# A two-layer decoder trunk: layers written out, one weight split moved ahead, another order of the first loads, a shorter last stage

## The chip, the cores and the metric

The kernel runs on one core of a Trainium2 chip. The time is the device time of one execution in microseconds (us); less is better. Five engines take part: TensorE (PE, matrix products into PSUM), VectorE (DVE), ScalarE (ACT), GpSimd (POOL) and SyncE (SP, which here only issues transfers). They run separate instruction streams and meet in semaphores.

## The reference

One inference step of a two-layer decoder for 256 prompt tokens and 8 sample tokens (264 columns in all), model width 1024, everything in float32:

```python
for l in range(2):
    h = h + 0.5 * rmsnorm(swiglu(rmsnorm(h, g1), wg1, wu1, wd1), p1)   # 1024 -> 2816 -> 1024
    a = rmsnorm(h, gm) @ w_in
    y = concat(conv_module(a), multiscale_pool(a), sparse_attention(a, caches)) @ w_out
    h = h + rmsnorm(y, pm)
    h = h + 0.5 * rmsnorm(swiglu(rmsnorm(h, g2), wg2, wu2, wd2), p2)
return h, new keys, values, conv and pool states of each layer
```

## The kernel before

**Data.** The activations stand transposed: `h[:, d, :]` is the residual, 128 features by 264 columns for each of eight `d`. The weights come as *units* of 128x1024 float32 (512 KB): 156 for each layer. A feed-forward part (ffn) uses 66 of them (22 gate and 22 up, in turns, then 22 down), the mixer 24.

**Three products for one.** A unit lands in `raw` (6 buffers). ACT copies it to `w_hi` in a rounded format, DVE computes `w_lo = raw - w_hi`; both have 3 buffers. This pair is called `split(L, u)`: it waits for the unit in `raw` and for PE to be done with the unit three earlier (`split_free`). PE then runs 24 matmuls per unit (`three`: x_hi·w_hi, x_lo·w_hi, x_hi·w_lo, for eight `d`).

**A stage.** Each of the six parts (ffn, mixer, ffn, twice) begins with `first_units` on PE: for each `d` in `ORDER` a column sum of squares and the products of the part's first two units. So PE works while `x_hi` (ACT), `x_lo` (DVE) and the squares `sq` come in. Meanwhile `rstd` becomes ready: ACT a square root from PSUM, DVE a reciprocal. In an ffn DVE then runs `gate(0)` (gs = product times rstd), ACT `silu(0)`, both the split of the fourth unit, `split(L, u0 + 3)`, DVE `up(0)`, and after them a loop of 7 rounds over the other units. POOL multiplies gate and up (`mid`).

**The end of a stage** is `post(L, n, ...)`: ACT squares the eight outputs, DVE adds them in pairs, PE sums them (`post_sums`) and then runs WARM = 9 products of constants; ACT takes the square root (`rms_post`), DVE the reciprocal and then for each `d` y = output * gain * rstd_post, POOL adds `h += y` (`add`), ACT and DVE make the next part's `x_hi`, `sq`, `x_lo` (`pre`, `pre_lo`). ACT and DVE also split two further units in `post`.

**Order.** On each engine the order is that in which the code is written. The loop over the layers is a loop on the chip (`Fori(0, DEPTH)`) on PE, ACT, DVE and POOL, in which semaphore values are computed from the register L (`at_layer`); on SP it is written out. The last layer therefore ends as any other: x_hi, x_lo, squares and column sums of a next layer are computed, three units (`TAIL`) behind the last one are loaded, and POOL reloads the parameters `pars`. At the end SP stores `h[:, d, :]` to `yT` as `h_new` counts up.

**The start.** SP issues `pars`, `h` as one transfer of 1056 KB, a table of ones, four units, three tables, two units. ACT waits for the first three of these (`inputs` at 48) and unit 0, splits units 0, 1, 2, and then makes the eight `x_hi` and `sq`.

Of the kernel before, what the change touches and what calls it, by code (L numbers as in the profile page):

```python
# [14 lines left out]
AL = mybir.AluOpType  # L15
ACT = mybir.ActivationFunctionType
# [5 lines left out]
NT = NP + NB  # L22
# [45 lines left out]
ORDER = (0, 1, 7, 2, 3, 4, 5, 6)  # L68
WARM = 9
# [19 lines left out]
    step=400,  # L89
# [6 lines left out]
def build(nc, xT, wts, par, cst, ptab, digits, kT, vC, kxT, scT, spT,  # L96
          yT, okT, ovT, okiT, ocP, ocS, opP, opS):
    ctx = ExitStack()
    with ctx:
# [119 lines left out]
        result = ctx.enter_context(nc.semaphore("result"))  # L219
        vx_full = ctx.enter_context(nc.semaphore("vx_full"))  # L220
# [22 lines left out]
        def _(sp):  # L243
# [37 lines left out]

            sp.dma_start(pars[:, :], par[0]).then_inc(inputs, 16)
            sp.dma_start(h[:, :, :], xT).then_inc(inputs, 16)
            sp.dma_start(con[:, C_ONE:C_COS], cst[:, C_ONE:C_COS]).then_inc(inputs, 16)
            for n in range(4):
                unit(n)
# [6 lines left out]
            for L in range(DEPTH):  # L293
                n = L * UNITS + RAW
                places = {}

                def read(*sequences):
                    for b in sequences:
                        places[b] = [page(g + b * NPG) for g in range(NPG)]


                with sp.Fori(0, NPG) as g:
                    for j in range(RAW):
                        unit(n + j, g)
# [24 lines left out]
                for q in range(KV):  # L329
                    batch(kT, L, q, places[2 * q + 1], "k_used", q + 1)  # L330

                sp.wait_ge(sem["unit_done"], at_layer(L, "unit_done", U_MIX + N_IN - 1))
                first_values(L, 0, places)
                spare_values(L, 2, places)
                batch(vC, L, 3, places[7], "k_used", KV + 4)

                sp.wait_ge(sem["v_used"], at_layer(L, "v_used", 2))
                for n in range(end, L * UNITS + U_FFN2):
                    unit(n)
                n = L * UNITS + U_FFN2  # L340
                last = (L + 1) * UNITS + (RAW if L + 1 < DEPTH else TAIL)
                with sp.Fori(0, (last - n) // RAW) as i:
                    for j in range(RAW):
                        unit(n + j, i)
                for n in range(last - (last - n) % RAW, last):
                    unit(n)

            for i, d in enumerate(ORDER):
                sp.wait_ge(sem["h_new"], at_layer(DEPTH - 1, "h_new", SIGNALS["h_new"] - KD + i + 1))
                sp.dma_start(yT[:, d, :], h[:, d, :]).then_inc(result, 16)  # L350
# [14 lines left out]
        def _(act):  # L365
# [22 lines left out]
            def post(L, n, nxt):  # L388
                for d in range(KD):
# [6 lines left out]
                    if d == 0:  # L396
                        act.activation(y[:, 0, :], PS[:, 0, 0:NT], ACT.Copy).then_inc(sem["y_out"], 1)
                    act.activation(sq[:, d, :], PS[:, d, 0:NT], ACT.Square).then_inc(sem["sq_post"], 1)
                split(L, (U_FFN, U_FFN2, UNITS)[n] + 1)
# [4 lines left out]
                               scale=four / D, bias=epsb[:, at:at + 1]).then_inc(sem["rms_post"], 1)  # L404
                pre(L, 8 * n, nxt, (U_FFN, U_FFN2, UNITS)[n] + 2)
                warm(1 + n, ACT.Tanh if n == 0 else ACT.Silu)

            def ffn(L, u0, f0):
# [8 lines left out]

                silu(0)
                split(L, u0 + 3)
# [13 lines left out]
                split(L, u0 + 66)  # L433
# [112 lines left out]
            act.wait_ge(inputs, 48)  # L546
            act.wait_ge(setup, 1)
            for u in range(TAIL):
                act.wait_ge(raw_full[u], 16)
                act.activation(w_hi[:, u, :], raw[:, u, :], ACT.Copy).then_inc(sem["w_hi"], 1)  # L550
            for d in ORDER:
                act.activation(x_hi[:, d, :], h[:, d, :], ACT.Copy,
                               scale=pars[:, PRE1 + d:PRE1 + d + 1]).then_inc(sem["x_hi"], 1)
                act.activation(sq[:, d, :], h[:, d, :], ACT.Square).then_inc(sem["sq_pre"], 1)  # L554
# [3 lines left out]
            with act.Fori(0, DEPTH) as L:  # L558
                ffn(L, 0, 0)
                post(L, 0, PREM)  # L560
                mixer(L)
                post(L, 1, PRE2)
                ffn(L, U_FFN2, KF)
                post(L, 2, PRE1N)
# [3 lines left out]
        def _(dve):  # L568
# [28 lines left out]
            def post(L, n, gain, nxt):  # L597
# [3 lines left out]
                split(L, (U_FFN, U_FFN2, UNITS)[n] + 1)  # L601
                dve.wait_ge(sem["rms_post"], at_layer(L, "rms_post", n + 1))
                after(L, step(L, dve.reciprocal(rstd_post[:, :], rstd_post[:, :])))

                for i in range(KD + 2):
# [10 lines left out]
            def ffn(L, n, u0, f0):  # L616
# [22 lines left out]
                dve.wait_ge(sem["rstd"], at_layer(L, "rstd", n))  # L639
                gate(0)  # L640
                split(L, u0 + 3)
# [14 lines left out]
                split(L, u0 + 66)  # L656
# [367 lines left out]
            dve.wait_ge(inputs, 48)  # L1024
            for u in range(TAIL):
                dve.wait_ge(raw_full[u], 16)
                dve.wait_ge(sem["w_hi"], u + 1)
                tt(w_lo[:, u, :], raw[:, u, :], w_hi[:, u, :].bitcast(F32), AL.subtract).then_inc(sem["w_lo"], 1)
            for i, d in enumerate(ORDER):
                dve.wait_ge(sem["x_hi"], i + 1)  # L1030
# [10 lines left out]
            with dve.Fori(0, DEPTH) as L:  # L1041
# [10 lines left out]
        def _(pe):  # L1052
# [19 lines left out]
            def post_sums(L, n):  # L1072
# [5 lines left out]

                pe.wait_ge(tables, 48)
# [360 lines left out]
            pe.wait_ge(inputs, 48)  # L1440
            with pe.Fori(0, DEPTH) as L:
# [6 lines left out]
            for i, d in enumerate(ORDER):  # L1448

                if i == 0:  # L1450
                    pe.wait_ge(sem["y_new"], at_layer(DEPTH, "y_new", 3 - KD))
                pe.wait_ge(sem["sq_pre"], DEPTH * SIGNALS["sq_pre"] + i + 1)
                pe.matmul(PS[:, 7, 0:NT], ones, sq[:, d, :],
                          start=(i == 0), stop=(i == KD - 1)).then_inc(sem["mm_pre"], 1)


        @block.gpsimd
        def _(pool):
# [11 lines left out]
            def add(L, n):  # L1470

                for i, d in enumerate(ORDER):
                    pool.wait_ge(sem["y_new"], at_layer(L, "y_new", 8 * n + i + 1))
# [11 lines left out]
            with pool.Fori(0, DEPTH) as L:  # L1485
# [45 lines left out]

                pool.wait_ge(sem["x_lo"], at_layer(L, "x_lo", 24))
# [126 lines left out]
```

## Time and profile before

| | |
|---|---|
| median of 3 runs | 1177.87 us (1174.03 to 1178.01) |
| the profiled execution: its own time | 1174.9 us |
| its span, first to last instruction | 1173.0 us |
| PE busy | 1095.5 us (93% of the span) |
| DVE, ACT, POOL busy | 757.0, 531.7, 209.2 us |
| mean granted TensorE clock | 0.980 of full |
| HBM read | 189.35 MB, 164 GB/s over the span |

The profile is one execution. The time of an engine in which it waits is given with what ended the wait; where nothing is seen that ended it, the row says "issue". Times in rows count from the start of the span. A matmul of 264 columns is shown with its pipelined duration (0.28 us at full clock, 0.42 at half); what counts is the distance between starts, 0.12 us at full clock.

### The profile page before, as it was taken

The numbers are of one execution on the slowest core, as the hardware profiler recorded it, in microseconds if no ns is written. First come the engines' busy times: TensorE is split into PE (matmuls) and PEld (weight loads), VectorE is DVE, ScalarE is ACT, GpSimd is POOL, SyncE is SP. The second block draws the span as 40 slices with busy tenths as digits, with TensorE's granted clock in tenths as the row PEclk, the third lists the DMA queues.
The fourth block names the chain that finished last, engine by engine and source line by source line (L and its number), as shares of the span: only waits on it lengthen the run. The fifth ranks groups of instructions, "written<-read, shape, count | busy, mean of one in ns | idle before, by whom it ended". The sixth has DMA issues, their size and how long they took to land.

```text
span 1173.0 us, 28793 instructions
## 1 busy us (share of the span) xinstructions
PE 1095.5 (93%) x9404; PEld 1034.2 (88%) x9404; DVE 757.0 (65%) x1250; ACT 531.7 (45%) x856; POOL 209.2 (18%) x245
## 2 busy tenths in 40 slices
PE   4999999999679999999989999999986799999997
PEld 4999999987458999999979999998864799999995
DVE  4666654689965666664466666448889466666546
ACT  5444433631444544443464444345215555444335
POOL 3112200411300221210041221004222022122002
PEclk9999999999979999999999999999998899999999
DMA  7445655443565355555434565563347535555541
GB/s 255 174 166 187 228 192 205 156 136 125 147 88 182 110 186 178 181 188 179 159 95 169 185 228 179 205 225 122 121 134 128 147 105 180 179 179 179 189 169 39
DMA packets 90506, 192.91 MB, mean 164 GB/s; under 512 B 12338, under 2 KB 48370, under 8 KB 90306
## 3 DMA queue, kind: packets, MB, share of 16 engines
q1 hardware_dynamic: 87426, 186.39, 49.1%
q0 software_dynamic: 3008, 5.60, 2.2%
q8 instruction: 40, 0.66, 0.3%
q14 instruction: 32, 0.26, 0.1%
HBM read 189.35 MB, written 2.59 MB: 164 GB/s over the span
## 4 chain that ended last, share of the span: by engine, by line
PE 50%; issue 39%; DVE 4%; POOLq 2%; ACT 2%; POOL 2%; DMA 1%; DVEq 0%; ACTq 0%; SPq 0%
PE PS L1055 14%; PE PS L1056 14%; PE PS L1057 14%; PE PS L1161 3%; PE PS L1089 2%; POOLq L1519 1%; POOL vx L1520 1%; PE PS L1104 1%; PE PS L1101 1%; PE PS L1100 1%; POOL h L1474 1%; ACT w_hi L369 1%; POOLq L1520 1%; DVE w_lo L576 1%; DVE wk L701 1%
## 5 line engine op out<-in xcount | busy, mean ns | idle before, releaser
L576 DVE TENSOR_TENSOR w_lo<-raw,w_hi 128x1024 fp32r<-128x1024 f32 x300 | 394.7, 1316 | 314.1 <-ACT w_hi L369 312.4
L1055 PE MATMUL PS<-x_hi,w_hi 128*128 128x264 f32 x1456 | 416.9, 286 | 10.5 <-DVE w_lo L576 10.5
L369 ACT ACTIVATE w_hi<-raw 128x1024 fp32r<-128x1024 f32 x300 | 315.6, 1055 | 242.9 <-PE PS L1057 219.0
L1056 PE MATMUL PS<-x_lo,w_hi 128*128 128x264 f32 x1456 | 414.6, 285 | 0.0
L1057 PE MATMUL PS<-x_hi,w_lo 128*128 128x264 f32 x1456 | 414.3, 285 | 0.0
L1055 PEld LDWEIGHTS PS<-x_hi,w_hi 128*128 128x128 f32 x1456 | 276.4, 190 | 11.7 <-DVE w_lo L576 11.3
L1056 PEld LDWEIGHTS PS<-x_lo,w_hi 128*128 128x128 f32 x1456 | 276.5, 190 | 0.1
L1057 PEld LDWEIGHTS PS<-x_hi,w_lo 128*128 128x128 f32 x1456 | 275.1, 189 | 0.0
L1055 PE MATMUL PS<-h_hi,w_hi 128*128 (+1 forms) x832 | 237.1, 285 | 3.4 <-issue 3.0
L1057 PE MATMUL PS<-h_hi,w_lo 128*128 (+1 forms) x832 | 236.9, 285 | 0.0
L1056 PE MATMUL PS<-h_lo,w_hi 128*128 (+1 forms) x832 | 236.1, 284 | 0.0
L1463 POOL TENSOR_TENSOR us<-gs,us 128x264 f32<-128x264 f32 x88 | 96.3, 1094 | 431.3 <-DVE us L628 431.3
L1055 PEld LDWEIGHTS PS<-h_hi,w_hi 128*128 128x128 f32 x832 | 156.5, 188 | 4.3 <-issue 4.3
L1056 PEld LDWEIGHTS PS<-h_lo,w_hi 128*128 128x128 f32 x832 | 157.0, 189 | 0.0
L1057 PEld LDWEIGHTS PS<-h_hi,w_lo 128*128 128x128 f32 x832 | 156.6, 188 | 0.0
L411 ACT ACTIVATE gs<-gs 128x264 f32<-128x264 f32 x88 | 37.3, 424 | 199.5 <-DVE gs L622 199.5
L1474 POOL TENSOR_TENSOR h<-h,y 128x264 f32<-128x264 f32 x48 | 41.6, 903 | 379.5 <-DVE y L608 379.5
L622 DVE TENSOR_TENSOR gs<-PS,rstd 128x264 f32<-128x264 f32 x88 | 38.0, 432 | 27.2 <-PE PS L1057 21.6
L1161 PE MATMUL PS<-x_all,raw 128*128 128x264 f32 x192 | 45.3, 389 | 0.0
L1089 PE MATMUL PS<-sq,con 128*128 128x264 f32 x96 | 30.8, 403 | 14.9 <-ACT sq L554 14.0
L1161 PEld LDWEIGHTS PS<-x_all,raw 128*128 128x128 f32 x192 | 35.7, 190 | 5.6
L636 DVE TENSOR_TENSOR h_lo<-us,h_hi 128x264 f32 x88 | 37.5, 426 | 0.0
(271 smaller groups left out, 1048.0 us busy)
## 6 DMA issues: line engine op xcount, KB each, us to landing
raw<-in_wts SPq DMA_DIRECT2D x315, 512.0 KB, 3.8
kv<-in_kT SPq DMA_DIRECT2D x128, 64.0 KB, 2.0
kx<-in_kxT SPq DMA_DIRECT2D x128, 32.0 KB, 2.1
vx<-in_vC POOLq DMA_DIRECT2D x48, 64.0 KB, 2.4
raw<-in_vC SPq DMA_DIRECT2D x48, 64.0 KB, 2.5
h<-in_xT SPq DMA_DIRECT2D x1, 1056.0 KB, 5.1
out_yT<-h SPq DMA_DIRECT2D x8, 132.0 KB, 1.7
vx<-in_vC SPq DMA_DIRECT2D x16, 64.0 KB, 9.0
```

Source lines behind the costliest of these rows:

```text
L369: act.activation(w_hi[:, u % SPLIT, :], raw[:, u % RAW, :], ACT.Copy) \
L411: act.activation(gs[:, f % 3, :], gs[:, f % 3, :], ACT.Silu).then_inc(sem["silu"], 1)
L576: tt(w_lo[:, u % SPLIT, :], raw[:, u % RAW, :], w_hi[:, u % SPLIT, :].bitcast(F32), AL.subtract) \
L622: tt(gs[:, f % 3, :], PS[:, 2 * (f % 3), 0:NT], rstd[:, :], AL.mult).then_inc(sem["gs"], 1)
L636: tt(out, us[:, f % 3, :], hi.bitcast(F32), AL.subtract).then_inc(sem["h_lo"], 1)
L1055: pe.matmul(out, w_hi[:, w, cols], hi, start=start, stop=False)
L1056: pe.matmul(out, w_hi[:, w, cols], lo, start=False, stop=False)
L1057: return pe.matmul(out, w_lo[:, w, cols], hi, start=False, stop=stop)
L1089: pe.matmul(PS[:, 7, 0:NT], ones, sq[:, ORDER[i], :], start=(i == 0), stop=(i == KD - 1)).then_inc(sem["mm_pre"], 1)
L1161: ins = pe.matmul(PS[:, m % 2, 0:NT], raw[:, (u0 + m) % RAW, col(k)], x_all[:, k, :], start=(k == 0), stop=(k == KD - 1))
L1463: pool.tensor_tensor(us[:, f % 3, :], gs[:, f % 3, :], us[:, f % 3, :], AL.mult).then_inc(sem["mid"], 1)
L1474: pool.tensor_tensor(h[:, d, :], h[:, d, :], y[:, d, :], AL.add).then_inc(sem["h_new"], 1)
```

## The change

The layer loop is written out on PE, ACT, DVE and POOL, so L is a constant (the inner loops stay). In each ffn the fourth unit is split ahead of silu(0) and gate(0), and the dummy activation that loads the silu table (`warm`) moves from `post` to behind that split. SP issues units 0 and 1 ahead of `h`, and `h` in four pieces with a semaphore each; unit 2 is split after the fifth `x_hi`. In the last layer nothing is prepared for a next one, and DVE adds three of the eight `h` (i = 2, 4, 6 in ORDER, which are d = 7, 3, 5) in POOL's place.

```diff
+BY_VECTOR = (2, 4, 6)
+PIECES = (slice(0, 2), slice(7, 8), slice(2, 4), slice(4, 7))
@@ SP
+            unit(0)
             sp.dma_start(pars[:, :], par[0]).then_inc(inputs, 16)
-            sp.dma_start(h[:, :, :], xT).then_inc(inputs, 16)
+            unit(1)
             sp.dma_start(con[:, C_ONE:C_COS], cst[:, C_ONE:C_COS]).then_inc(inputs, 16)
-            for n in range(4):
+            for i, piece in enumerate(PIECES):
+                sp.dma_start(h[:, piece, :], xT[:, piece, :]).then_inc(h_in[i], 16)
+            for n in range(2, 4):
                 unit(n)
...
-                last = (L + 1) * UNITS + (RAW if L + 1 < DEPTH else TAIL)
+                last = (L + 1) * UNITS + (RAW if L + 1 < DEPTH else 0)
@@ ACT
-                split(L, (U_FFN, U_FFN2, UNITS)[n] + 1)
+                last = n == 2 and L == DEPTH - 1
+                if not last:
+                    split(L, (U_FFN, U_FFN2, UNITS)[n] + 1)
...
+                if last:
+                    return
                 pre(L, 8 * n, nxt, (U_FFN, U_FFN2, UNITS)[n] + 2)
-                warm(1 + n, ACT.Tanh if n == 0 else ACT.Silu)
+                if n == 0:
+                    warm(3, ACT.Tanh)
...
+                split(L, u0 + 3)
+                warm(1 + f0 // KF, ACT.Silu)
                 silu(0)
-                split(L, u0 + 3)
...
-            act.wait_ge(inputs, 48)
             act.wait_ge(setup, 1)
-            for u in range(TAIL):
+            warm(0, ACT.Sqrt)
+            for u in range(TAIL - 1):
                 act.wait_ge(raw_full[u], 16)
                 act.activation(w_hi[:, u, :], raw[:, u, :], ACT.Copy).then_inc(sem["w_hi"], 1)
+            act.wait_ge(inputs, 32)
             for d in ORDER:
+                if d == 4:
+                    act.wait_ge(raw_full[TAIL - 1], 16)
+                    act.activation(w_hi[:, TAIL - 1, :], raw[:, TAIL - 1, :], ACT.Copy).then_inc(sem["w_hi"], 1)
+                act.wait_ge(h_in[PIECE_OF[d]], 16)
...
-            with act.Fori(0, DEPTH) as L:
+            for L in range(DEPTH):
@@ DVE
+                if last:
+                    for i, d in enumerate(ORDER):
+                        ins = stt(y[:, d, :], PS[:, d, 0:NT] if d else y[:, d, :], pars[:, gain + d:gain + d + 1],
+                                  rstd_post[:, :], AL.mult, AL.mult)
+                        ins.then_inc(sem["y_new"], 1)
+                        if i - 1 in BY_VECTOR:
+                            d = ORDER[i - 1]
+                            dve.wait_ge(sem["y_new"], at_layer(L, "y_new", 8 * n + i))
+                            tt(h[:, d, :], h[:, d, :], y[:, d, :], AL.add).then_inc(sem["h_last"], 1)
+                    return
...
                 dve.wait_ge(sem["rstd"], at_layer(L, "rstd", n))
+                split(L, u0 + 3)
                 gate(0)
-                split(L, u0 + 3)
                 up(0)
@@ PE
-            with pe.Fori(0, DEPTH) as L:
+            for L in range(DEPTH):
...
-            for i, d in enumerate(ORDER):
-                if i == 0:
-                    pe.wait_ge(sem["y_new"], at_layer(DEPTH, "y_new", 3 - KD))
-                pe.wait_ge(sem["sq_pre"], DEPTH * SIGNALS["sq_pre"] + i + 1)
-                pe.matmul(PS[:, 7, 0:NT], ones, sq[:, d, :], ...)
@@ POOL
+                    if n == 2 and L == DEPTH - 1 and i in BY_VECTOR:
+                        continue
...
+                if L == DEPTH - 1:
+                    break
                 pool.wait_ge(sem["x_lo"], at_layer(L, "x_lo", 24))
                 pool.dma_start(pars[:, :], par[bass.ds(L + 1, 1)].rearrange("a p n -> (a p) n")).then_inc(pars_full, 16)
```

The rows of an engine's program are shown as line, operation, output<-inputs, and the semaphores that it waits for. On ACT, at the head of the first layer's first ffn, before (the square root, the layer loop's entry, silu, the fourth unit's split with the registers that its waits need, and the inner loop's entry):

```order
L556 ACTIVATE rstd<-PS,epsb 128x264 [waits mm_pre]
L558 UNCONDITIONAL_BRANCH
L558 ISA
L411 ACT_TABLE_LOAD
L411 ACTIVATE gs<-gs 128x264 [waits gs]
L356 ISA
L361 ISA [waits raw_full3]
L369 ACTIVATE w_hi<-raw 128x1024 [waits unit_done]
L420 UNCONDITIONAL_BRANCH
```

and in the change:

```order
L579 ACTIVATE rstd<-PS,epsb 128x264 [waits mm_pre]
L380 ACTIVATE w_hi<-raw 128x1024 [waits unit_done,raw_full3]
L385 ACT_TABLE_LOAD
L385 ACTIVATE junk<-epsb 128x1
L427 ACTIVATE gs<-gs 128x264 [waits gs]
L437 UNCONDITIONAL_BRANCH
```

The split of the unit in `raw_full3` moved ahead of the table load and of silu, and the branch and register rows of the layer loop are gone. On DVE, at the end of the program, before (from the reciprocal of the last `post` on):

```order
L603 RECIPROCAL rstd_post<-rstd_post 128x264 [waits rms_post]
L595 REGISTER_ALU
L608 SCALAR_TENSOR_TENSOR y<-y,pars,rstd_post 128x264 [waits step]
L608 SCALAR_TENSOR_TENSOR y<-PS,pars,rstd_post 128x264 x2
L582 REGISTER_ALU
L583 SCALAR_TENSOR_TENSOR x_lo<-h,pars,x_hi 128x264 [waits x_hi]
...
L576 TENSOR_TENSOR w_lo<-raw,w_hi 128x1024 [waits w_hi]
L613 REGISTER_ALU
L614 RECIPROCAL rstd<-rstd 128x264 [waits rms_pre]
L1041 REGISTER_ALU
L1041 COMPARE_AND_BRANCH
```

and in the change:

```order
L628 RECIPROCAL rstd_post<-rstd_post 128x264 [waits rms_post]
L632 SCALAR_TENSOR_TENSOR y<-y,pars,rstd_post 128x264 [waits step]
L632 SCALAR_TENSOR_TENSOR y<-PS,pars,rstd_post 128x264 x3
L638 TENSOR_TENSOR h<-h,y 128x264 [waits y_new]
L632 SCALAR_TENSOR_TENSOR y<-PS,pars,rstd_post 128x264 x2
L638 TENSOR_TENSOR h<-h,y 128x264 [waits y_new]
L632 SCALAR_TENSOR_TENSOR y<-PS,pars,rstd_post 128x264 x2
L638 TENSOR_TENSOR h<-h,y 128x264 [waits y_new]
```

Eight `x_lo`, a split and a reciprocal are gone, and three adds to `h` stand between the `y`. On SP, at the start of the program, before:

```order
L282 DMA pars<-in_par 128x126
L283 DMA h<-in_xT 128x2112
L284 DMA con<-in_cst 128x128
L253 DMA raw<-in_wts 128x1024 x4
L287 DMA con<-in_cst 128x640
```

and in the change:

```order
L257 DMA raw<-in_wts 128x1024
L287 DMA pars<-in_par 128x126
L257 DMA raw<-in_wts 128x1024
L289 DMA con<-in_cst 128x128
L291 DMA h<-in_xT 128x528
L291 DMA h<-in_xT 128x264
L291 DMA h<-in_xT 128x528
L291 DMA h<-in_xT 128x792
L257 DMA raw<-in_wts 128x1024 x2
L294 DMA con<-in_cst 128x640
```

Two units (512 KB each) moved ahead of `h`, and `h` became four transfers of 264, 132, 264 and 396 KB.

## Rows read from the trace of the kernel before

**Rows 1.** Stretches: us, us, PE, PEld, DVE, ACT, POOL busy (instructions), PEclk, DMA.

```profile
35.00:218.00 183.00, 182.34 (x1497) 181.75 (x1496) 107.53 (x129) 83.52 (x115) 22.20 (x21) 1.00 0.55 195
...
325.00:379.00 54.00, 44.35 (x421) 37.85 (x422) 30.90 (x55) 25.95 (x50) 0.25 (x1) 0.88 0.58 131
```

**Rows 2.** Waits of PE: waiting, released by, total us, times, longest.

```profile
PE PS L1089 <- ACT sq L554: 14.0, 1, 14.0
...
PE PS L1055 <- DVE w_lo L576: 10.5, 4, 4.6
```

**Rows 3.** Timeline, ACT, DVE, PE, start of the first layer's second ffn.

```profile
390.36 0.48 ACT L385 ACTIVATE rstd<-PS,epsb 128x264 f32<-128x264 f32 x1 [1.87 <-PE PS L1089]
390.86 1.28 ACT L374 ACT_TABLE_LOAD   x1
...
393.17 0.42 ACT L411 ACTIVATE gs<-gs 128x264 f32<-128x264 f32 x1 [0.82 <-DVE gs L622]
393.50 1.99 ACT L369 ACTIVATE w_hi<-raw 128x1024 fp32r<-128x1024 f32 x2
...
390.87 1.80 DVE L614 RECIPROCAL rstd<-rstd 128x264 f32<-128x264 f32 x1 [1.13 <-ACT rstd L385]
392.71 0.43 DVE L622 TENSOR_TENSOR gs<-PS,rstd 128x264 f32<-128x264 f32 x1
394.58 1.23 DVE L576 TENSOR_TENSOR w_lo<-raw,w_hi 128x1024 fp32r<-128x1024 f32 x1 [1.44 <-ACT w_hi L369]
...
395.86 0.39 PE L1055 MATMUL PS<-x_hi,w_hi 128*128 128x264 f32 x1 [1.92 <-DVE w_lo L576]
```

**Rows 4.** Timeline, ACT, DVE, PE, start of the second layer.

```profile
600.87 1.28 ACT L411 ACT_TABLE_LOAD   x1 [2.17 <-issue]
...
601.67 0.43 DVE L622 TENSOR_TENSOR gs<-PS,rstd 128x264 f32<-128x264 f32 x1 [2.65 <-issue]
...
604.84 0.59 PE L1055 MATMUL PS<-x_hi,w_hi 128*128 128x264 f32 x1 [4.56 <-DVE w_lo L576]
```

**Rows 5.** Stretches of 3.4 us after PE's waits at three ffn starts (columns of rows 1).

```profile
30.90:34.30 3.40, 3.40 (x18) 3.40 (x17) 1.96 (x3) 1.68 (x3) 1.32 (x1) 0.50 0.74 220
...
604.40:607.80 3.40, 2.96 (x13) 2.96 (x14) 2.20 (x4) 1.24 (x3) 1.66 (x1) 0.51 0.50 153
970.10:973.50 3.40, 3.40 (x28) 3.40 (x29) 1.96 (x4) 1.65 (x4) 1.67 (x1) 1.00 0.63 170
```

**Rows 6.** Transfers issued at 2.41 and 3.72 (KB, us to landing); timeline of the start.

```profile
raw<-in_wts SPq DMA_DIRECT2D x1, 512.0 KB, 6.4
...
raw<-in_wts SPq DMA_DIRECT2D x1, 512.0 KB, 8.4
...
2.41 2.33 SPq L253 DMA_DIRECT2D raw<-in_wts  x4
8.88 1.28 ACT L550 ACT_TABLE_LOAD   x1 [8.88 <-DMA raw<-in_wts]
10.18 3.04 ACT L550 ACTIVATE w_hi<-raw 128x1024 fp32r<-128x1024 f32 x3
13.98 1.25 PE L1089 MATMUL PS<-sq,con 128*128 128x264 f32 x2 [13.98 <-ACT sq L554]
...
17.37 0.28 PE L1101 MATMUL PS<-x_hi,w_lo 128*128 128x264 f32 x1
```

**Rows 7.** Timeline of DVE in the first mixer: two small operations, each waiting for the last.

```profile
267.26 0.15 DVE L733 TENSOR_SCALAR rad<-rad 128x1 f32<-128x1 f32 x1
267.44 0.15 DVE L734 TENSOR_SCALAR rad<-rad 128x1 f32<-128x1 f32 x1
```

**Rows 8.** Timeline of the end (DVE, POOL), and the stores of yT (KB, us to landing).

```profile
1156.22 1.79 DVE L603 RECIPROCAL rstd_post<-rstd_post 128x264 f32<-128x264 f32 x1
...
1158.62 6.91 POOL L1474 TENSOR_TENSOR h<-h,y 128x264 f32<-128x264 f32 x8 [67.64 <-DVE y L608]
1167.32 0.58 POOL L1533 DMA_DIRECT2D pars<-in_par  x1 [1.79 <-DVE x_lo L583]
...
out_yT<-h SPq DMA_DIRECT2D x8, 132.0 KB, 1.7
```

More of the change, by code:

```diff
@@ L68 @@
 ORDER = (0, 1, 7, 2, 3, 4, 5, 6)
+BY_VECTOR = (2, 4, 6)
+PIECES = (slice(0, 2), slice(7, 8), slice(2, 4), slice(4, 7))
+PIECE_OF = {0: 0, 1: 0, 7: 1, 2: 2, 3: 2, 4: 3, 5: 3, 6: 3}
 WARM = 9
@@ L88 @@
     pool_y=1, pl_hi=1, pl_lo=1, pl_ohi=1, pl_olo=1,
-    step=400,
+    h_last=3, step=400,
 )
@@ L219, in build @@
         result = ctx.enter_context(nc.semaphore("result"))
+        h_in = [ctx.enter_context(nc.semaphore(f"h_in{i}")) for i in range(len(PIECES))]
         vx_full = ctx.enter_context(nc.semaphore("vx_full"))
@@ L348, in _ @@
             for i, d in enumerate(ORDER):
-                sp.wait_ge(sem["h_new"], at_layer(DEPTH - 1, "h_new", SIGNALS["h_new"] - KD + i + 1))
+                if i in BY_VECTOR:
+                    sp.wait_ge(sem["h_last"], BY_VECTOR.index(i) + 1)
+                else:
+                    sp.wait_ge(sem["h_new"], at_layer(DEPTH - 1, "h_new", SIGNALS["h_new"] - KD + 1 + i - sum(
+                        j < i for j in BY_VECTOR)))
                 sp.dma_start(yT[:, d, :], h[:, d, :]).then_inc(result, 16)
@@ L432, in ffn @@
                 warm(4 + f0 // KF, ACT.Sqrt)
-                split(L, u0 + 66)
+                if u0 + 66 < UNITS or L + 1 < DEPTH:
+                    split(L, u0 + 66)
             def mixer(L):
@@ L600, in post @@
                     tt(sq[:, d, :], sq[:, d, :], sq[:, d + 1, :], AL.add).then_inc(sem["y_sum"], 1)
-                split(L, (U_FFN, U_FFN2, UNITS)[n] + 1)
+                last = n == 2 and L == DEPTH - 1
+                if not last:
+                    split(L, (U_FFN, U_FFN2, UNITS)[n] + 1)
                 dve.wait_ge(sem["rms_post"], at_layer(L, "rms_post", n + 1))
                 after(L, step(L, dve.reciprocal(rstd_post[:, :], rstd_post[:, :])))
+                if last:
[8 more added lines that the diff above has]
+                    return
                 for i in range(KD + 2):
@@ L655, in ffn @@
                         split(L, u0 + k, i)
-                split(L, u0 + 66)
+                if u0 + 66 < UNITS or L + 1 < DEPTH:
+                    split(L, u0 + 66)
             def mixer(L):
@@ L1023, in _, with first_split @@
             dve.sem_inc(sem["y_new"], FIRST["y_new"])
-            dve.wait_ge(inputs, 48)
-            for u in range(TAIL):
+            def first_split(u):
                 dve.wait_ge(raw_full[u], 16)
@@ L1028, in _ @@
                 tt(w_lo[:, u, :], raw[:, u, :], w_hi[:, u, :].bitcast(F32), AL.subtract).then_inc(sem["w_lo"], 1)
+            for u in range(TAIL - 1):
+                first_split(u)
+            dve.wait_ge(inputs, 32)
             for i, d in enumerate(ORDER):
+                if d == 5:
+                    first_split(TAIL - 1)
+                dve.wait_ge(h_in[PIECE_OF[d]], 16)
                 dve.wait_ge(sem["x_hi"], i + 1)
@@ L1040, in _ @@
                                 owned[:, q])
-            with dve.Fori(0, DEPTH) as L:
+            for L in range(DEPTH):
+                steps[0] = 0
                 ffn(L, 0, 0, 0)
@@ L1077, in post_sums @@
                 ins.then_inc(sem["mm_post"], 1)
+                if n == 2 and L == DEPTH - 1:
+                    return
                 pe.wait_ge(tables, 48)
@@ L1438, in mixer @@
                     ins.then_inc(sem["unit_done"], 1)
-            pe.wait_ge(inputs, 48)
-            with pe.Fori(0, DEPTH) as L:
+            pe.wait_ge(inputs, 32)
+            for L in range(DEPTH):
                 ffn(L, 0, 0, 0)
@@ L1447, in _ @@
                 post_sums(L, 2)
-            for i, d in enumerate(ORDER):
-                if i == 0:
-                    pe.wait_ge(sem["y_new"], at_layer(DEPTH, "y_new", 3 - KD))
-                pe.wait_ge(sem["sq_pre"], DEPTH * SIGNALS["sq_pre"] + i + 1)
-                pe.matmul(PS[:, 7, 0:NT], ones, sq[:, d, :],
-                          start=(i == 0), stop=(i == KD - 1)).then_inc(sem["mm_pre"], 1)
         @block.gpsimd
@@ L1484, in _ @@
             pool.wait_ge(setup, 1)
-            with pool.Fori(0, DEPTH) as L:
+            for L in range(DEPTH):
                 pool.dma_start(stc[:, :, :, 0:CK - 1], scT[bass.ds(L, 1)].rearrange("a p c b k -> p (a c) b k")) \
```

## The prediction

> **What bounds the kernel now.** I first read the table of stretches. In the long loops of an ffn PE is busy 182.34 of 183 us and starts 1497 matmuls [rows 1], one each 0.12 us: nothing beside PE counts there, and the change leaves those loops as they are. In the second half of a mixer PE is busy 44.35 of 54 us [rows 1]; other engines matter there. Next I read the list of PE's waits. Two entries lie where the change works: 14.0 us at the start, ended by ACT's first squares, and 10.5 us in four waits for `w_lo` of L576, the longest 4.6 [rows 2]. By the timeline these four are the heads of the four ffns (waits of 2.1, 1.9, 4.6 and 1.9 us). Last I read the rows of the start, of the second layer's start and of the end. The reader is to see who is late in each, below.
>
> **The ffn heads.** In [rows 3] ACT has `rstd` at 390.84, loads a table, waits for DVE's `gs`, runs silu at 393.17 and only then copies the fourth unit (two copies in 1.99 from 393.50). DVE's difference follows at 394.58 for 1.23, and PE starts at 395.86 after a wait of 1.9 (all in the group): it was free at 393.96. In the change the copy comes right after `rstd`: 390.9 to 391.9, and DVE's difference right after its reciprocal (390.87 + 1.80 = 392.7) ends at 393.9. PE waits 0 to 0.1. What is late next is the fifth unit: gs at 393.9 to 394.3, silu to 394.8 (the table load, 390.9+1.0+1.28, is over by 393.5 and costs nothing while DVE is busy), copy to 395.8, difference to 397.05. PE's unit of 24 x 0.12 = 2.9 us started at 393.95 ends at 396.85: it waits 0.2, and by the same sum 0.2 again for the sixth. After that the loop has the order that it has now, where PE doesn't wait. So 0.4 us are left at each head, and 0.4 more at the first, where four small copies stand on DVE between reciprocal and split: 2.0 of 10.5. Gain **8.5**.
>
> The third head needs the written-out loop too. There ACT and DVE each stand 2.17 and 2.65 us with nothing seen that ends it ("issue"), at the point where the layer loop jumps back, and ACT loads the silu table a second time [rows 4]. Without a jump I expect the same 0.4 there as elsewhere. Were the stop to stay, about 2.6 us of it would.
>
> After three of the four waits PE's granted clock is 0.50 for 3.4 us, its lower level (1.2 GHz): 18 matmuls start in the first such stretch, 17 in the second (at 396.10), 13 in the third, of which PE is busy 2.96; after the fourth wait, at the upper level, 28 do [rows 5]. Missing are 10 + 11 + 11 = 32 matmuls of 0.12 us, **3.9** us. Each fall stands behind a wait of 1.9 us or more, and I expect no wait over 0.5 to be left, so I take all of it; the bound below is 0.
>
> **The start.** Unit 0 is issued at 2.41 and lands 6.4 later, at 8.8; unit 2, issued at 3.72, lands at 12.1 [rows 6]. So 1.65 us per 512 KB while transfers queue. Ahead of unit 0 stand 63 + 1056 + 64 KB, 2.3 units, so the flow begins near 8.8 - 3.3 x 1.65 = 3.4. In the new order unit 0 lands at 5.0, unit 1 (with pars) at 6.9, the ones at 7.1, the pieces of `h` at 7.9, 8.3, 9.2 and 10.5, and unit 2, behind the same bytes as before, at 12.1. ACT's table load (8.88 now, after the wait for data) lies in the wait. ACT copies unit 0 to 6.1, unit 1 to 7.9, DVE's difference of unit 1 (1.23) ends at 9.2 and is the last thing that PE needs: ACT's first x_hi and squares (0.9) are ready at 8.8. PE starts at 9.2 instead of 13.98: 4.8 earlier. The copy of unit 2 stands ahead of the sixth x_hi (12.1 + 1.0 + 0.5 = 13.6), which PE reaches at about 16.7 by its present pace: 3 us of cover. The tables behind, units 4 and 5, and all from unit 6 on keep their times; DMA is busy 0.55 in the loops [rows 1], and I count no later cost. From this I take 0.8 off for the clock: PE's matmuls have their short form from 17.37 on, 3.4 us after the first [rows 6], and when the clock rises is not in the kernel's hand; if it rises up to 3.4 us later than that, up to 1.6 us are lost, and I take half. Gain **4.0** (bounds 2 and 5.5).
>
> The Trainium skill ("TensorE: Matmul & The Clock Gate", What's actually happening) says that what watches PE's activity runs freely and does not restart with the kernel, so that the moment of the rise differs from run to run; the trace has one start and cannot show that. By that rule nothing is sure of the 0.8 but its bounds.
>
> The pieces of `h` are the other point. [Rows 6] show no fixed cost for each transfer beyond the flow: 1.65 us for each of two queued units. The same skill ("DMA: Bandwidth & Descriptors", Measured) advises transfers of 1 MiB or more and gives 0.95 us for 64 KB against 6.15 for 1 MB, which speaks against cutting `h`. By an estimate between those two figures the first piece takes 2.0 us instead of 0.85, PE would start about 0.8 later, and the sum would be 1152.3 instead of 1151.5. The rows of this trace decide for me.
>
> **The end.** DVE's last `rstd_post` reciprocal starts at 1156.22; POOL's eight adds run from 1158.62 to 1165.53, 0.86 each; behind them x_hi, x_lo, a split, and POOL's load of `pars`, issued at 1167.32 for 0.58; if it lands 1.7 later, as the stores do, that is 1169.6, and the span ends at 1173.0, 3.4 after that [rows 8]. In the change the split ahead of the reciprocal is gone (0.2). DVE then has 8 y and 3 adds at about 0.41, so the last y, the tenth, ends near 1161.9; POOL's fifth add ends at 1162.8, SP's store lands 1.7 later at 1164.5. With the same tail of 3.4 behind POOL's last work the span ends at 1166.2. Gain **6.8**. Bounds: the tail vanishes and the store decides (1164.5, gain 8.5), or the tail counts from the store's landing (1167.9, gain 5.1).
>
> **The rest of the written-out layers.** Register instructions disappear outside the inner loops. In the mixer DVE's dependent small operations start 0.18 apart at 0.15 each [rows 7]: at most 0.03 lies between them, with a register instruction for each wait, so these run in the shadow. The trace doesn't show what a handover between engines would save. Bounds: 0 below (a constant is no slower than a register), 1.5 us per mixer above; I take 0.5 each, near the row. Gain **1.0** (0 to 3). WARM, `pre_sum` and the rest of `first_units` are unchanged: PE itself sets their pace.
>
> **Sum.** 8.5 + 3.9 + 4.0 + 6.8 + 1.0 = 24.2 us, from 1174.9, the profiled execution's own time (span 1173.0), to 1150.7. The median of the three runs shown lies 3.0 above that execution; the same gain from it gives 1153.7. I put the forecast between them, nearer the profile: **1151.5 us**.
>
> **Rivals.**
> - *The heads only move their wait* (0.11). The fifth or sixth unit is late by 1 to 2 us, because ACT's table load falls between copy and silu, and PE's clock still falls. For it: ACT has four jobs in a row there. Against: DVE's 1.80 + 1.23 cover the table load. It gives back 3.9 and some 3 us: 1158.5.
> - *The start is lost again* (0.08): the earlier PE meets units that come as before, or the pieces arrive late. Against: units 6 to 8 are issued before PE needs them, and a unit takes 1.65 to arrive and 2.9 to be used. 1155.5.
> - *The mixers gain more than the bound* (0.10): each handover is shorter by a register instruction, and less of the 9.6 us that PE stands in 54 [rows 1] is left. 3 us per mixer: 1146.5.
> - *Slower* (0.02): code. PE's program grows from 1595 rows to 2937, and every layer is new code. If each engine stood 2.2 to 2.65 us as in [rows 4] each time code comes in, some 12 such stops on the path of PE, 30 us, would eat the gain and 0.5% more: 1184. It decides from 12 stops on. Against: the first layer runs the same rows for the first time now, and its loops show PE busy throughout [rows 1]; the stops stand where the loop jumps.
> - *Nothing of note* (0.03): two of the terms fail together, the heads and the start, and the mixers lose by another phase of the clock: above 1172.
> - The forecast holds the other 0.66; its own range is 1147 to 1156.
>
> **Numbers.** A measurement of this kernel can tell about 0.5% (5.9 us) from no change. The range 1145.5 to 1158.5 takes in the forecast's bounds, the mixer case and the start case; outside stay most of the first rival and the last two. Faster 0.95, same 0.03, slower 0.02.
>
> **What would show it.** PE's wait for `sq` of 14.0 becomes 9 to 9.5. The four waits for `w_lo` of 10.5 sum to under 2.5, none over 0.5 to 0.8, and no clock of 0.5 stands behind an ffn head. No row of ACT or DVE at the second layer's start has 2 us of "issue". POOL's last add ends 7 us before today's, and the span ends 3 to 3.5 us after it. DVE's small operations in the mixers stay 0.18 apart. I am wrong if the fifth unit's `w_lo` releases PE after more than 1 us, if PE starts after 11 us, if POOL's tail behind the last add is over 5 us, or if the mixers change by more than 3 us either way.

## The result and the profile after

The change takes 1166.34 us (median of 4 runs, 1163.8 to 1166.81) where the kernel before takes 1177.63 on the same chip: ratio 0.9915, 95% interval 0.9895 to 0.9934. It is faster: the medians lie 11.3 us apart and the ratio stands for 10.0 us. The forecast was a gain of 24. The profiled execution of the change has a span of 1162.1 us, 10.9 less than before.

The list of PE's waits (waiting, released by, total us, times, longest), with which the prediction began:

```profile
PE PS L1343 <- DMA kv<-in_kT: 17.1, 2, 9.5
PE PS L1420 <- DVE dg L1022: 11.0, 2, 5.5
PE PS L1134 <- DVE w_lo L1063: 9.6, 1, 9.6
...
PE PS L1098 <- DVE w_lo L599: 0.2, 1, 0.2
```

The start's 14.0 of [rows 2] is 9.6, and the 10.5 us for `w_lo` at the ffn heads are down to 0.2, the last row. But the list has a new head: 17.1 us in two waits for a transfer into `kv`. Before, the same line (the key products, then L1298) waited 0.2 us for it.

Where the time went is plain from the starts of the column sums at the end of each part (`post_sums`). The stretches between them, in us, for the kernel before, the change, and the first experiment below (stores held back):

| from one part's column sums to the next | before | change | held back |
|---|---|---|---|
| start of the span to the first ffn's | 215.21 | 208.14 | 208.24 |
| mixer, layer 0 | 159.40 | 164.50 | 157.75 |
| second ffn, layer 0 | 206.25 | 203.21 | 203.20 |
| first ffn, layer 1 | 208.76 | 203.23 | 203.24 |
| mixer, layer 1 | 159.16 | 166.96 | 158.97 |
| second ffn, layer 1 | 204.73 | 203.32 | 203.22 |
| from the last ones to the end | 19.45 | 12.78 | 12.79 |

Outside the mixers the change gains 7.07 + 3.04 + 5.53 + 1.41 + 6.67 = 23.7 us; the prediction's terms for these are 8.5 + 3.9 + 4.0 + 6.8 = 23.2. The mixers, for which it had a gain of 1.0, lose 5.1 + 7.8 = 12.9. The stretches of the two mixers in the change (columns of [rows 1]):

```profile
208.14:372.64 164.50, 136.34 (x1445) 112.11 (x1444) 123.47 (x306) 64.92 (x135) 35.35 (x49) 0.95 0.48 129
779.08:946.04 166.96, 136.75 (x1444) 112.26 (x1443) 123.47 (x306) 64.92 (x135) 35.35 (x49) 0.93 0.47 127
```

and in the kernel before:

```profile
215.21:374.61 159.40, 137.62 (x1444) 112.59 (x1443) 123.83 (x306) 64.94 (x135) 35.09 (x49) 0.95 0.49 133
789.62:948.78 159.16, 138.40 (x1444) 113.75 (x1443) 123.90 (x306) 64.95 (x135) 35.01 (x49) 0.95 0.50 133
```

Every engine does the same work, in nearly the same busy time. The mixers have only become longer.

**The new wait.** PE's timeline in the first mixer of the change (start, us, operation; in brackets the idle time before it):

```profile
316.47 0.87 PE L1399 MATMUL PS<-con,sp__108 128*128 128x128 f32 x6
324.92 3.45 PE L1343 MATMUL PS<-kv,LA 128*32 128x512 f32 x16 [7.57 <-DMA kv<-in_kT]
```

The key transfers that SP issues from 300 to 330 in the change, and in the kernel before (the second row of each is the time from issue to landing):

```profile
L264 SPq DMA_DIRECT2D kv<-in_kT x31: 345/380/1247, 299.7 to 315.8; - x31
...
DMA to landing us min/median/max: 1.8/2.1/9.0
```

```profile
L260 SPq DMA_DIRECT2D kv<-in_kT x32: 345/368/1267, 306.5 to 323.0; - x32
...
DMA to landing us min/median/max: 1.8/2.1/3.3
```

SP issues the last of them 7.2 us earlier than before, just as much as the layer is ahead; but it lands 9.0 us after its issue (315.80 to 324.8). What is new around 315? POOL's timeline in the change and before:

```profile
313.44 0.53 POOL L1559 DMA_DIRECT2D vx<-in_vC  x1 [0.73 <-issue]
314.09 0.68 POOL L1563 DMA_DIRECT2D out_opP<-pp  x1
314.67 1.28 POOL L1564 DMA_DIRECT2D out_opS<-stp  x1
```

```profile
322.57 0.54 POOL L1520 DMA_DIRECT2D vx<-in_vC  x1 [0.83 <-issue]
323.38 0.68 POOL L1524 DMA_DIRECT2D out_opP<-pp  x1 [0.28 <-issue]
323.96 1.28 POOL L1525 DMA_DIRECT2D out_opS<-stp  x1
```

POOL stores the pool state (`opP`, `opS`) 9.3 us earlier, not 7.2: opS is now issued 1.1 us ahead of SP's last key transfer, and was 0.9 us behind it. In the second layer it was 0.07 behind (898.18 against 898.11) and is 2.9 ahead (885.55 against 888.48). The 2 us come from POOL's inner loop of 24 value loads ahead of the stores. The groups of POOL from 280 to 330 (count | busy, mean ns | idle before), before and in the change:

```profile
L1520 POOL DMA_DIRECT2D vx<-in_vC x24 | 12.9, 539 | 22.1 <-issue 22.1
```

```profile
L1559 POOL DMA_DIRECT2D vx<-in_vC x24 | 12.9, 537 | 20.3 <-issue 20.3
```

The loads themselves take as long; between them POOL stands 0.08 us less each, since with a constant L less is worked out for the address. The register instructions of that line, from 280 to 330, before and in the change (count: ns min/median/max):

```profile
L1520 POOLq FUSED_REGOPS  x32: 47/127/158, 288.5 to 321.8; - x32
```

```profile
L1559 POOLq FUSED_REGOPS  x24: 64/64/93, 281.6 to 312.8; - x24
```

From the store of `okiT` to that of `opP` it is 35.86 us before and 33.85 in the change.

### The profile page after: what moved, and what is told of

It reads as the page before. It is cut to its first block, busy times and chain, and to the rows that moved or that the text cites. A ratio compares the mean times of both kernels' runs of the same rounds, so it can differ in the third digit from the quotient of the medians.

```text
span 1162.1 us, 27694 instructions
## 1 busy us (share of the span) xinstructions
PE 1079.9 (93%) x9370; PEld 1023.2 (88%) x9370; DVE 751.7 (65%) x1241; ACT 517.9 (45%) x834; POOL 191.1 (16%) x241
## 3 DMA queue, kind: packets, MB, share of 16 engines
q0 software_dynamic: 2976, 5.53, 2.2%
## 4 chain that ended last, share of the span: by engine, by line
PE 81%; DVE 8%; ACT 3%; issue 2%; SPq 2%; DMA 2%; POOL 0%; DVEq 0%; POOLq 0%; ACTq 0%
PE PS L1098 23%; PE PS L1099 23%; PE PS L1100 23%; SPq L264 2%; PE PS L1134 2%; PE PS L1206 2%; DMA kv<-in_kT 2%; PE PS L1229 1%; DVE w_lo L599 1%; PE PS L1146 1%; PE PS L1145 1%; PE PS L1149 1%; PE PS L1343 1%; DVE rstd_post L628 1%; ACT w_hi L380 1%
## 5 line engine op out<-in xcount | busy, mean ns | idle before, releaser
L1500 POOL TENSOR_TENSOR us<-gs,us 128x264 f32<-128x264 f32 x88 | 81.0, 921 | 430.8 <-DVE us L663 399.9
L1513 POOL TENSOR_TENSOR h<-h,y 128x264 f32<-128x264 f32 x45 | 38.8, 893 | 397.6 <-DVE y L643 329.6
```

Source lines behind the costliest of these rows:

```text
L1500: pool.tensor_tensor(us[:, f % 3, :], gs[:, f % 3, :], us[:, f % 3, :], AL.mult).then_inc(sem["mid"], 1)
L1513: pool.tensor_tensor(h[:, d, :], h[:, d, :], y[:, d, :], AL.add).then_inc(sem["h_new"], 1)
```

## The experiments

The theory: written out, POOL's loop is 2 us shorter, so opS (120 KB in 2048 pieces of 60 bytes) goes ahead of SP's last key loads and blocks the DMA engines for them, and PE waits. The rivals: SP's own value loads crowd the keys; the wait only holds the surplus that arrives early, and another would take its place; another store or the bytes as such do it; or the earlier start and heads bring it about, not POOL's loop. All runs were timed against the kernel before on the same chip. The chips differ from experiment to experiment, and the median of the kernel before with them (1174.65, 1175.27 and 1177.49 us), so between experiments a ratio says more than a difference of microseconds.

**Stores held back** (`after_hold`), in the change:

```diff
                 pool.wait_ge(sem["pool_c"], at_layer(L, "pool_c", 1))
+                pool.wait_ge(sem["k_used"], at_layer(L, "k_used", 8))
                 pool.dma_start(opP[...
```

> The changed kernel, with POOL's two pool-state stores (opP, opS) held back until PE is done with the second key products (one wait more on k_used ahead of them). My theory: in the changed kernel opS overtakes the last key transfers of SP, which land 9 us after their issue and not 2, and PE waits 7.5 and 9.5 us for them. Then this kernel has no such wait (under 1 us in both layers together), each mixer takes about 159.4 us from column sums to column sums as before the change and not 164.5 and 167.0, and the time is about 12.9 us below the changed kernel: 1153.4 (1151 to 1156), ratio to the kernel before 0.979. Rival one, SP's own value loads fill the lanes and opS is a bystander: the wait stays at 14 us or more and the time at 1166. Rival two, the wait is only the surplus of work that now arrives early, and another wait (for DVE's dg or the values) takes its place: the kv wait is gone but the time falls by under 4 us, 1162 to 1166.

Measured: 1149.64 us (1149.1 to 1152.09) against 1174.65, ratio 0.979 (0.9778 to 0.9803). PE's timeline at the second keys:

```profile
317.71 1.92 PE L1343 MATMUL PS<-kv,LA 128*32 128x512 f32 x16 [0.26 <-DMA kv<-in_kT]
```

The wait of 7.57 is 0.26, and the products run in 1.92 us, not 3.45, since the clock has not fallen. The mixers take 157.75 and 158.97 us (last column of the table), a little less than the 159.4 that was expected; all else is as in the change. The time lies below the expected 1151 to 1156, but the kernel before was also faster on this chip, and the ratio is the 0.979 that was put. Both rivals fall: with the value loads where they were the wait goes. Other waits take back little of it: those for `h_lo` grow from 1.8 to 4.2 us and those for `spm` from 2.8 to 4.1, and the two mixers together are 14.7 us shorter. One line gives 1.25% more, and this is the fastest of all the kernels here that compute everything.

**The same wait in the kernel before** (`before_hold`, same edit).

> The kernel before, with the same wait ahead of the stores as in the first run. Its stores already come 0.3 to 0.9 us behind SP's last key issue, and its wait for keys is 0.2 us. My theory: no change in the time, 1176.5 to 1178.5, ratio 0.999 to 1.001. Rival, the stores cost the kernel before something too (the values or the units behind are late): 2 to 6 us faster, 1172 to 1175.

Measured: 1174.70 against 1174.65, ratio 1.0004 (0.9996 to 1.0013). Before the change the stores cost nothing where they are, behind the last keys. That is not because opS blocks nothing there. The loads beside it, from 320 to 340 in the kernel before (KB each, median us to landing):

```profile
vx<-in_vC SPq DMA_DIRECT2D x8, 64.0 KB, 8.8
...
kv<-in_kT SPq DMA_DIRECT2D x7, 64.0 KB, 2.1
...
out_opS<-stp POOLq DMA_DIRECT2D x1, 120.0 KB, 11.5
```

The value loads behind opS are as late as the keys are in the change, but no wait of PE for them shows.

**POOL's layer loop alone written out** (`before_pool`), in the kernel before:

```diff
-            with pool.Fori(0, DEPTH) as L:
+            for L in range(DEPTH):
```

> The kernel before, with the layer loop written out on POOL alone. My theory: POOL's loop of 24 value loads gets shorter by some 0.1 us a load, its stores come 2 to 2.6 us earlier against SP's key loads, and PE's wait for the last keys (0.2 us before) appears: 4 to 8 us in each mixer, so 1177.6 + 13 = 1190 (1184 to 1193), ratio 1.010. Rival one, the wait comes from all that the change does upstream (earlier start, heads), not from POOL's loop: 1177 to 1178, ratio 1.000. Rival two, the other engines' written-out code makes the difference: also 1.000, with POOL's stores as far behind SP's last key issue as before.

Measured: 1186.67 us, ratio 1.0078 (1.0048 to 1.0108), slower. opS is issued at 321.09 where SP's last key goes at 322.38, and PE's waits show

```profile
PE PS L1298 <- DMA kv<-in_kT: 12.6, 2, 6.9
```

So neither the earlier start, nor the heads, nor the other engines' code is needed: this single line of code, on an engine that is 18% busy, costs 12 us. Of its six runs five are at 1186.0 to 1187.3 and one at 1175.2. That fits a race between the two queues that is now and then still won, but no trace of that run shows it.

**Without opS** (`after_noS`), in the change:

```diff
-                pool.dma_start(out4(opS), stp[:, :, :, 1:]).then_inc(stored, 16)
...
-                pool.wait_ge(stored, L * 112 + 112)
+                pool.wait_ge(stored, L * 96 + 96)
```

> The changed kernel without the store opS (the sample tokens' pool state is left out of the output); opP and all other transfers stay where they are. My theory, opS with its 60-byte pieces is what blocks the lanes: the last keys land about 2 us after their issue, PE's wait for them is under 1 us a layer, and the time is 1153 (1150 to 1156). Rival, opP or the sheer number of transfers in flight does it: wait and time stay at over 10 us and 1163 to 1166.

Measured: 1150.84 us (1149.52 to 1151.55), ratio 0.9794 (0.9781 to 0.9806). With opP at its early place 1.8 us of waits for `kv` are left of 17.1. It is opS. Whether the 1.8 are opP's part (with both stores held back 0.3 are left) was not tried.

**opS in whole rows** (`after_whole`), in the change:

```diff
-                pool.dma_start(out4(opS), stp[:, :, :, 1:]).then_inc(stored, 16)
+                pool.dma_start(opS[bass.ds(L, 1)].rearrange("a p c b k -> (a p) (c b k)"), con[:, 0:2 * NB * PB]).then_inc(stored, 16)
```

> The changed kernel without the wait ahead of the stores. opS is issued at the same place, on the same queue, with the same 120 KB to the same tensor, but from a table whose 240 values of a partition lie side by side, so that it is 128 pieces of 960 bytes and not 2048 of 60 (what is stored is not the pool state). My theory, the small pieces block the lanes: the wait for the last keys is gone (under 1 us), time 1150 (1149 to 1153). Rival, any store from this queue at this point does it, by its bytes or its queue: the wait stays at 14 us or more and the time at 1163 to 1167. In between, if opP (256 pieces of 60 bytes) has a part, 1 to 3 us of wait.

Measured: 1150.53 us (1149.63 to 1150.7), ratio 0.9784 (0.9771 to 0.9798). The issues of POOL and SP from 312 to 326 (KB each, median us to landing), in this kernel:

```profile
kv<-in_kT SPq DMA_DIRECT2D x9, 64.0 KB, 2.3
vx<-in_vC SPq DMA_DIRECT2D x8, 64.0 KB, 2.0
raw<-in_vC SPq DMA_DIRECT2D x8, 64.0 KB, 1.9
...
out_opS<-con POOLq DMA_DIRECT2D x1, 120.0 KB, 3.7
```

and in the change:

```profile
kv<-in_kT SPq DMA_DIRECT2D x8, 64.0 KB, 2.4
vx<-in_vC SPq DMA_DIRECT2D x8, 64.0 KB, 7.5
raw<-in_vC SPq DMA_DIRECT2D x7, 64.0 KB, 3.8
...
out_opS<-stp POOLq DMA_DIRECT2D x1, 120.0 KB, 11.5
```

The same bytes, on the same queue, at the same moment: 3.7 us in pieces of 960 bytes, 11.5 in pieces of 60, and the transfers of SP beside them land in 3.1 us at most, not in up to 9.0. PE's waits for `kv` are 3.0 us together, more than the 1 us of the theory, less than the 17.1 of the change; it is what was put for the case that opP, still in pieces of 60 bytes, has a part. The small pieces block, not the bytes or the queue.

**The terms of the prediction, one undone at a time**, each on the kernel with the stores held back (1149.64). The start (`hold_oldstart`): `pars` and `h` whole ahead of the units, units 0 to 2 split ahead of all x_hi.

```diff
-            unit(0)
             sp.dma_start(pars[:, :], par[0]).then_inc(inputs, 16)
-            unit(1)
+            sp.dma_start(h[:, :, :], xT).then_inc(inputs, 16)
...
-            for i, piece in enumerate(PIECES):
-                sp.dma_start(h[:, piece, :], xT[:, piece, :]).then_inc(h_in[i], 16)
-            for n in range(2, 4):
+            for n in range(4):
```

> The changed kernel with the stores held back (1149.6 us in its run), and the order of the first transfers and of the first splits as before. By my prediction the new start is worth 4.0 (bounds 2 and 5.5): 1153.6. The traces so far show PE's first wait as 9.8 in place of 14.2 and the first half of the layer 6.5 us shorter, of which 2 to 2.5 belong to the first head: 4.0 to 4.5, so 1153.5 to 1154.2. Rival: the earlier start is mostly lost again, under 2 us, 1150 to 1151.5.

Measured: 1153.31 us (1152.61 to 1154.65), 3.7 more than `after_hold`, which ran on another chip; up to the first column sums 212.20 against 208.24 us, 4.0 more.

The heads (`hold_oldheads`):

```diff
-                split(L, u0 + 3)
-                warm(1 + f0 // KF, ACT.Silu)
                 silu(0)
+                split(L, u0 + 3)
...
-                split(L, u0 + 3)
                 gate(0)
+                split(L, u0 + 3)
```

> The changed kernel with the stores held back, and at the ffn heads the old order: silu and gate ahead of the fourth unit's split, and the table load in the post part. By my prediction the heads' waits are worth 8.5, of which the part of the third head that belongs to the layer loop's jump (about 2.6) is not undone here, and the clock behind them 3.9 where it falls: 1149.6 + 5.9 + 0 to 3.9 = 1155.5 to 1159.5, with four waits of about 1.9 to 2.1 us for w_lo. Rival: with constants in place of registers the old order would have waited less, under 1 us a head: 1150 to 1153.

Measured: 1157.79 us (1157.14 to 1160.08), 8.2 more, with these waits:

```profile
PE PS L1096 <- DVE w_lo L597: 8.3, 4, 2.2
```

The end (`hold_oldend`): no `last` on ACT and DVE, no early return on PE, no skip and no break on POOL, three units more on SP.

> The changed kernel with the stores held back, and the last layer ending as any other, as in the kernel before. By my prediction this end costs 6.8 (5.1 to 8.5): 1156.4; the traces so far give 6.7 from the last column sums to the end of the span. Rival: part of the 6.7 comes from the written-out code and stays, so 1153 to 1155.

Measured: 1156.71 us (1155.97 to 1156.84), 7.1 more; from the last column sums to the end of the span 19.1 against 12.8 us.

**The written-out loop by itself**, on PE, ACT, DVE and POOL in the kernel before, with the stores held back (`unroll_hold`) and without (`unroll_only`), and **the change itself again** (`after_again`):

> The kernel before with the layer loop written out on PE, ACT, DVE and POOL and the stores held back; heads, start and end as before the change. If the parts add up (start 3.7, heads 8.1, end 7.1 undone from 1149.6), it takes 1168.5 (1167 to 1170.5), 6.1 below the kernel before at 1174.7. My prediction's terms for this part, 1.0 for the mixers and 2.6 for the stop at the second layer's start, would give 1171. Rival: the parts overlap and the loop alone is worth under 2 us: 1173 to 1175.

> The same without the wait ahead of the stores. My theory: the written-out loop on POOL brings the waits for the last keys, as in the kernel with POOL alone written out (1186.7, +12.0 over before): 1168.5 + 12 to 16 = 1180.5 to 1184.5, ratio 1.005 to 1.009, slower than before. Rival: with PE, ACT and DVE written out too, SP's key transfers come earlier by as much as POOL's stores and there is no wait: 1168 to 1171.

> The changed kernel itself, unchanged, on the same chip as the two others: ratio 0.9915 (0.9895 to 0.9934) to the kernel before, with 17 us of waits for the last keys. With 1174.7 for the kernel before, 1163 to 1167.

Measured, against 1177.49 for the kernel before: 1169.43 (1166.95 to 1170.52), ratio 0.992 (0.9892 to 0.9949); 1185.01 (1177.22 to 1186.2), ratio 1.0054 (1.0029 to 1.0079); 1167.30 (1165.48 to 1170.51), ratio 0.9905 (0.9875 to 0.9935). With the stores held back the loop is worth 8.1 us by these medians and 9.4 by the ratio, but its profile is only 4.3 shorter than that of `before_hold` (1168.2 against 1172.5): 3.6 less in the first ffn of the second layer (the jump, and a fall of the clock), 1.3 less in the last ffn (another fall), and the two mixers together 0.8 more. If the stores stay where they are the loop costs 15.6: alone it makes the kernel slower. The 6.1 of the expectation is what the other parts leave of the 25.0 between 1174.65 and 1149.64 and so can't confirm the sum. The ratios can: start, heads and end undone cost 0.22, 0.57 and 0.50% (0.9812, 0.9847 and 0.984 against 0.979), the loop by itself gives 0.80%, together 2.09 of the 2.10% of all, with 0.1 to 0.3 of uncertainty in each. The first wait of `unroll_only`:

```profile
PE PS L1299 <- DMA kv<-in_kT: 19.8, 2, 10.2
```

## Why the prediction was wrong

**The heads** (8.5, right). The start of the first layer's second ffn in the change, for [rows 3] (ACT, DVE, PE):

```profile
388.54 0.48 ACT L396 ACTIVATE rstd<-PS,epsb 128x264 f32<-128x264 f32 x1 [1.94 <-PE PS L1134]
...
389.06 1.80 DVE L649 RECIPROCAL rstd<-rstd 128x264 f32<-128x264 f32 x1 [1.09 <-ACT rstd L396]
...
389.20 1.06 ACT L380 ACTIVATE w_hi<-raw 128x1024 fp32r<-128x1024 f32 x1 [0.18 <-PE PS L1149]
...
390.28 1.28 ACT L385 ACT_TABLE_LOAD   x1
...
390.89 1.23 DVE L599 TENSOR_TENSOR w_lo<-raw,w_hi 128x1024 fp32r<-128x1024 f32 x1
```

The copy stands ahead of the table load, DVE's difference right behind its reciprocal, and it is over at 392.12; PE takes up the fourth unit at 392.17, 0.33 us after the start of its last product where 0.12 would be without a stop. An ffn takes 203.2 us, against 205.0 with the old order and a wait of 2.02: 0.2 to 0.3 us are left at a head, where the forecast left 0.4 to 0.8. The stop of 2.17 and 2.65 us at the second layer's start [rows 4] is gone, and with the old order in a written-out loop all four waits are about 2.1 (8.3 together), so the jump cost 2.2 to 2.6, as put.

**The clock behind the heads** (3.9, right in sum, its condition too simple). In the change no stretch behind a head is at the lower level. But a wait of 2 us does not always bring it: with the old heads and held-back stores, three stretches behind waits of 2.19, 2.02 and 2.02 us,

```profile
25.80:29.20 3.40, 3.40 (x18) 3.40 (x19) 1.96 (x4) 1.65 (x3) 1.59 (x1) 0.58 0.54 183
391.70:395.10 3.40, 3.40 (x16) 3.40 (x17) 1.96 (x4) 1.68 (x3) 1.57 (x1) 0.51 0.64 196
598.20:601.60 3.40, 3.40 (x28) 3.40 (x29) 1.96 (x4) 1.68 (x4) 1.59 (x1) 1.00 0.60 179
```

and in `unroll_hold`, behind waits of 2.20 and 2.02:

```profile
31.20:34.60 3.40, 3.40 (x28) 3.40 (x29) 1.96 (x4) 1.64 (x4) 1.60 (x1) 1.00 0.60 173
395.10:398.50 3.40, 3.40 (x28) 3.40 (x29) 1.96 (x4) 1.63 (x4) 1.58 (x1) 1.00 0.51 172
```

The same wait gives 0.51 once and 1.00 another time. A fall costs 1.5 us (an ffn takes 206.5 us with one and 205.0 without). The Trainium skill ("TensorE: Matmul & The Clock Gate", What's actually happening) has the watcher run on its own time, not that of the kernel; these rows agree. A term for the clock should be a chance times 1.5 us, not all falls or none. That the profiled execution before had three falls, and so gave about the forecast's 3.9, is luck: `before_hold`, with the same heads, has two, and `unroll_hold` none.

**The start** (4.0, right: 3.7 by the medians, 4.0 by the stretch). For [rows 6]:

```profile
4.62 1.06 ACT L568 ACTIVATE w_hi<-raw 128x1024 fp32r<-128x1024 f32 x1 [1.30 <-DMA raw<-in_wts]
...
7.16 1.06 ACT L568 ACTIVATE w_hi<-raw 128x1024 fp32r<-128x1024 f32 x1 [1.48 <-DMA raw<-in_wts]
...
8.32 1.23 DVE L1063 TENSOR_TENSOR w_lo<-raw,w_hi 128x1024 fp32r<-128x1024 f32 x1 [1.31 <-ACT w_hi L568]
...
9.64 1.22 PE L1134 MATMUL PS<-sq,con 128*128 128x264 f32 x2 [9.64 <-DVE w_lo L1063]
```

The last thing that PE needs is the difference of unit 1, as said; it ends at 9.55 where 9.2 was put, and PE starts at 9.64 in place of 13.98. The pieces of `h` land at 8.12, 8.73, 9.28 and 10.80, where 7.9, 8.3, 9.2 and 10.5 were put: the first 0.2 late, and not by the 1.15 (2.0 in place of 0.85) of the estimate against cutting `h`. The clock rises at 14.0, 4.4 us later (3.4 before).

**The end** (6.8, right: 6.67 by the stretch, 7.1 by the medians). POOL's last add in the change, for [rows 8]:

```profile
1158.01 0.86 POOL L1513 TENSOR_TENSOR h<-h,y 128x264 f32<-128x264 f32 x1 [0.28 <-DVE y L632]
```

It ends at 1158.87, 7.0 after the start of DVE's reciprocal at 1151.85 (6.8 was put, from 1156.02 to 1162.8), and the span at 1162.1, 3.3 later (3.4 was put).

**The rest of the written-out layers** (1.0, bounds 0 to 3). This step failed. It priced registers by DVE's small operations in the mixers [rows 7] and set the lower bound at 0, "a constant is no slower than a register". For the engines' own speed the small term may stand: DVE's small operations are still 0.18 apart (260.39 and 260.57), and with the stores held back the mixers take 157.5 to 159.3 us in the four changed kernels, 158.9 and 160.6 in `unroll_hold`, and 159.2 to 159.5 before. No gain clear of that spread is shown; of the 1.65 us in the first mixer of `after_hold` 1.33 lie in the key products, which met the upper clock there (1.92 us) and the lower one before (3.25). But it is no bound for the kernel, since it asks only how fast an engine is and not what else moves with it. The one loop that the constants shorten much is POOL's value loop, by 2.0 us of 35.9 in each mixer, and what stands behind that loop is a store that must not come ahead of SP's last keys. The margin was 0.93 and 0.07 us, and no view of it was taken. So the mixers lost 12.9 us instead of gaining 1.0, far outside the 3 us either way that the prediction named as its sign of being wrong; the other terms came out 0.5 above their 23.2, and that makes up the 13.3 between the sum (24.2) and the profiles (10.9). Put back, the kernel takes 1149.64, 25.0 below the one before; the sum was 24.2. None of the rivals named this: the one called slower spoke of stops where new code comes in, of which no run shows any sign, and the one of nothing of note had the mixers lose by the phase of the clock.

**How opS blocks.** In the trace's DMA records of the change opS is 32 packets of 3840 bytes, that is 64 pieces of 60 bytes in each. Between 315 and 316 us a 512-byte packet of SP's queue takes 0.027 us (291 of them in 7.99); between 320 and 321 it takes 0.40 (39 in 15.66). The Trainium skill ("DMA: Bandwidth & Descriptors", Queues, rings and completion order) says that a DMA engine goes round its queues by packets and takes all pieces of one packet, 64 at most, before it turns to the next queue. The packets of 64 pieces agree with that, but turns alone don't account for the delay. The 32 packets begin from 317.15 to 318.47 and their records end by 320.97, 15.0 us in all on 16 engines, while SP's 512-byte packets still take 0.18 us each from 321 to 323, 0.12 from 323 to 324, and opS lands at 326.1. In the second layer the records end at 891.97, SP's packets take 0.11 to 0.17 us each until 897, and opS lands at 897.5. What holds them up behind the packets' records, the writes of opS perhaps, is open.

## What to carry to other kernels

An edit that makes an engine off the path faster moves the transfers behind it: list what that engine issues, on which side of the critical queue's last transfer it falls, and by what margin; here margins of 0.07 and 0.93 us decided over 14.7 us. Hold a store that nobody waits for behind the last load that somebody waits for, by a semaphore and not by timing, or give it long pieces (960 bytes instead of 60: 3.7 us instead of 11.5). And when a change of several parts gives less than its sum, compare stretches between fixed points first: one table showed five parts that had gained and two that had lost.

## What the runs showed of the hardware that was not expected

- A store of 120 KB in 60-byte pieces from POOL's queue makes 64 KB loads of SP's queue land after up to 9.6 us, where their median is 2.1 without it. Beside the same bytes in 960-byte pieces they take 3.1 at most (waits of PE 17.1 and 3.0 us). SP's packets stay slow for 3 to 5 us after the last record of the store's own packets (320.97 and 891.97).
- POOL stands 0.08 us less between two transfers with addresses from the inner loop when the outer loop's index is a constant.
- After the same wait of 2.02 us PE's clock is at 0.51 in one place and at 1.00 in another; one fall costs 1.5 us.
- One kernel had two times: 1186.0 to 1187.3 in five runs, 1175.2 in the sixth. The race is the likely cause, but not shown.
